# Two row groups of the array at once: spreads of the mLSTM maxima and neighbourhood scores issued in pairs

## The reference, cut to what matters

```python
# neighbourhood attention: 4 heads of 64; local scores with bias beside scores on the context
s_loc = jnp.einsum('bwhd,biwjhd->bhwij', q_r, k_win)
s_ctx = jnp.einsum('bwhd,bchd->bhwc', q_r, k_ctx)
s = jnp.concatenate([s_loc * scale + bias, s_ctx * scale], axis=-1)
p = jax.nn.softmax(s, axis=-1)

# mLSTM, 4 heads, forwards and backwards
d_log = jnp.where(tri, b[..., :, None] - b[..., None, :] + ic[..., None, :], -jnp.inf)
inter = b + m[..., None]
m_t = jnp.maximum(inter, jnp.max(d_log, axis=-1))
s = jnp.einsum('bhtk,bhsk->bhts', qc, kc) * jnp.exp(d_log - m_t[..., None])
num = a[..., None] * jnp.einsum('bhvk,bhtk->bhtv', C, qc) + jnp.einsum('bhts,bhsv->bhtv', s, vc)
h = num / jnp.maximum(jnp.abs(den), jnp.exp(-m_t))[..., None]
```

## Time and profile before

| | before |
|---|---|
| median of 3 runs | 1969.7 us (1965.51 to 1973.23) |
| the profiled execution | 1965.12 us |
| its span | 1963.2 us |
| TensorE busy | 1693.0 us, 86% |
| VectorE, ScalarE, GpSimd busy | 547.5, 325.3, 96.3 us |
| mean granted TensorE clock | 0.935 |

### The profile page before, as it was taken

The page is one execution under the profiler, slowest core; times in us unless marked ns, Lnnn a source line. Parts: engine busy times, 40 slices in busy tenths (PEclk is TensorE's granted clock), DMA queues, the critical chain, the costliest instruction groups (busy, mean ns, idle before and its releaser), DMA issues.

```text
span 1963.2 us, 21642 instructions
## 1 busy us (share of the span) xinstructions
PE 1693.0 (86%) x9155; PEld 881.1 (45%) x9155; DVE 547.5 (28%) x1054; ACT 325.3 (17%) x776; POOL 96.3 (5%) x171
## 2 busy tenths in 40 slices
PE   6999999999997998979888799999997766576765
PEld 2656444444476432424222266857885323222222
DVE  2145044354664121112111523334113111011102
ACT  4113143200023100101001321243012000000001
POOL 5000110000021100000000000110000000000000
PEclk9999999999998999999999899999998877777776
DMA  9310104544576799999999931104766999999995
GB/s 345 116 44 22 16 1 193 215 153 147 172 303 229 283 405 421 421 421 421 421 421 421 391 124 57 32 7 132 249 242 264 421 422 421 421 420 420 421 420 246
DMA packets 130668, 525.17 MB, mean 268 GB/s; under 512 B 9886, under 2 KB 73532, under 8 KB 75276
## 3 DMA queue, kind: packets, MB, share of 16 engines
q1 hardware_dynamic: 127884, 520.47, 67.1%
q0 software_dynamic: 2688, 3.32, 0.9%
HBM read 522.70 MB, written 1.05 MB: 267 GB/s over the span
## 4 chain that ended last, share of the span: by engine, by line
PE 60%; DMA 33%; DVE 4%; ACT 1%; issue 1%; SPq 0%; DVEq 0%; ACTq 0%
DMA ring<-in_w_e_dram 33%; PE ps L813 13%; PE ps L1073 9%; PE ps L1253 8%; PE ps L1082 4%; PE ps L1112 4%; PE ps L1037 3%; PE ps L723 2%; PE ps L1275 2%; PE ps L999 2%; PE ps L1205 2%; PE ps L915 2%; PE ps L1233 2%; PE ps L1021 1%; PE ps L892 1%
## 5 line engine op out<-in xcount | busy, mean ns | idle before, releaser
L1253 PE MATMUL ps<-ring,arena 128*32 128x256 f32 (+1 forms) x2880 | 381.1, 511 | 111.7 <-DMA ring<-in_w_e_dram 108.6
L1253 PEld LDWEIGHTS ps<-ring,arena 128*32 128x32 f32 (+1 forms) x2880 | 124.8, 130 | 354.1 <-DMA ring<-in_w_e_dram 179.7
L1275 PE MATMUL ps<-ring,arena 128*32 128x256 f32 (+1 forms) x1472 | 216.2, 564 | 74.0 <-DMA ring<-in_w_e_dram 70.3
L1073 PE MATMUL ps<-arena,ring 128*128 128x512 f32 (+1 forms) x576 | 191.8, 486 | 0.0
L813 PE MATMUL ps<-arena,ring 128*128 128x512 f32 (+1 forms) x480 | 175.2, 523 | 1.4 <-DVE arena L1828 1.4
L1275 PEld LDWEIGHTS ps<-ring,arena 128*32 128x32 f32 (+1 forms) x1472 | 69.6, 141 | 216.4 <-issue 111.0
L2054 DVE COPY arena<-ps 32x512 f32<-32x512 f32 (+1 forms) x128 | 70.9, 554 | 271.0 <-PE ps L1275 269.7
L1617 ACT ACTIVATE arena<-ps 128x512 f32<-128x512 f32 (+1 forms) x32 | 15.7, 490 | 777.1 <-PE ps L1253 777.1
L1073 PEld LDWEIGHTS ps<-arena,ring 128*128 128x128 f32 x576 | 109.1, 190 | 76.1 <-issue 68.6
L813 PEld LDWEIGHTS ps<-arena,ring 128*128 128x128 f32 x480 | 90.2, 190 | 82.5 <-issue 76.6
L2047 DVE TENSOR_TENSOR arena<-arena,ps 128x512 f32<-128x512 f32 (+1 forms) x32 | 17.7, 554 | 368.8 <-PE ps L1253 368.8
(11 more groups left out here) (215 smaller groups left out, 1435.3 us busy)
## 6 DMA issues: line engine op xcount, KB each, us to landing
ring<-in_w_e_dram SPq DMA_DIRECT2D x364, 1024.0 KB, 17.8
ring<-in_w_in_dram SPq DMA_DIRECT2D x44, 1024.0 KB, 9.0
ring<-in_w_mod_dram SPq DMA_DIRECT2D x40, 1024.0 KB, 11.2
arena<-in_w_e_dram SPq DMA_DIRECT2D x17, 1024.0 KB, 7.1
ring<-in_w_out_dram SPq DMA_DIRECT2D x8, 1024.0 KB, 11.4
arena<-in_w_mod_dram SPq DMA_DIRECT2D x8, 1024.0 KB, 14.7
arena<-in_w_br_ml_dram SPq DMA_DIRECT2D x8, 512.0 KB, 6.1
arena<-in_w_br_mla_dram SPq DMA_DIRECT2D x8, 256.0 KB, 3.9
```

The source lines that it names most:

```text
L1073: mm = pe.matmul(ps[:, u % 3, tq], wg[:, k, cols], hT[:, k, tq], start=k == 0, stop=k == KD - 1)
L1253: mm = pe.matmul(ps[M * j:M * j + M, m, 0:NW], XSTs[l][e // GROUP % 2][:, kk, e % GROUP, 0:M], w[:, k, j * NW:(j + 1) * NW], start=kk == 0 ...
L1275: mm = pe.matmul(ps[M * j:M * j + M, 3, 0:NW], lhs, w[:, k, j * NW:(j + 1) * NW], start=kk == 0, stop=kk == KD - 1)
```

## The change

Only TensorE's program changes. In the mLSTM loop `spread_m` now issues both directions of a head, each as a matmul over its own 32 rows instead of 64, one behind the other; a head's two spreads stand in front of the wait for `p_ready` of the odd map before, behind that map's projection. In the attention loop the MLA half keeps its order; in the neighbourhood half the scores of two heads are issued one behind the other (rows 0 to 63 and 64 to 127 of the array), then the two turns of the pair before, then the gate products of both units, then the values of the pair before. Both scores of a pair wait for both exponentials of the pair before.

```diff
                 def spread_m(u):
-                    h, d = L.pairs[u]
                     if u >= 2:
-                        pe.wait_ge(sem("e1_ready"), before("e1_ready", l) + 4 * (u - 1))
-                    r = 32 * d + h
-                    pe.matmul(ps[:, 3 + d, tq], ident[0:64, r:r + 1].to_broadcast([64, P]), R3[0:64, 2, tq],
-                              start=True, stop=True).then_inc(sem("nm_ready"), 1)
+                        pe.wait_ge(sem("e1_ready"), before("e1_ready", l) + 4 * u)
+                    h = L.pairs[u][0]
+                    for d in range(2):
+                        at = 32 * d
+                        pe.matmul(ps[:, 3 + d, tq], ident[at:at + 32, at + h:at + h + 1].to_broadcast([32, P]),
+                                  R3[at:at + 32, 2, tq], start=True, stop=True).then_inc(sem("nm_ready"), 1)
...
                 spread_m(0)
-                spread_m(1)
                 for u, (h, d) in enumerate(L.pairs):
...
+                    if d == 1 and u + 1 < len(L.pairs):
+                        spread_m(u + 1)
                     pe.wait_ge(sem("p_ready"), before("p_ready", l) + u + 1)
                     if d == 1 and h + 1 < HEADS:
                         scores_ml(h + 1)
                     values_ml(u)
-                    if u + 2 < len(L.pairs):
-                        spread_m(u + 2)
...
-                for i in range(nu + 2):
-                    if i < nu:
+                half = nu // 2
+                for i in range(half + 1):
+                    if i < half:
                         score(i)
-                    if i < nu:
                         gate_products(6 * KD * i // nu, 6 * KD * (i + 1) // nu)
-                    if 1 <= i <= nu:
+                    if i >= 1:
                         turn(i - 1)
                     if i >= 3 and i % 2:
                         values(i - 3)
+                for i in range(half, nu + 2, 2):
+                    if i < nu:
+                        pe.wait_ge(sem("attn_exp"), before("attn_exp", l) + i)
+                        score(i)
+                        score(i + 1)
+                    if i > half:
+                        turn(i - 2)
+                        turn(i - 1)
+                    if i < nu:
+                        gate_products(6 * KD * i // nu, 6 * KD * (i + 2) // nu)
+                    values(i - 2)
```

## The result

The changed kernel takes 1996.6 us (median of 4 runs, 1992.0 to 2000.3), the kernel before, on the same chip, 1968.1. The ratio is 1.015, 95% interval 1.0132 to 1.0169: slower by 28 us, where the forecast was +8 and the range ended at 1987. The profiled execution has a span of 1990.2 us, 27.0 over that of before, at a mean granted clock of 0.921 (0.935 before).

The account below looks back on a forecast made before the run. TensorE was taken to bound the kernel, transfers following it. mLSTM +7.2 and +6.5, attention -3.6 and -5.9, clock +4 sum to +8.2 on 1965.1: 1973.3, or 1978 for the median; range 1969 to 1987.

Parts of the forecast that it names:

- the overlap: Spreads and scores: two matmuls on different row groups run fully side by side, a spread pair costing 1.05 us.
- Rival 2: Paired matmuls don't overlap, 1983 us (chance 0.13), or take three passes of four, 1980.5 us (0.07).
- the stall, its place and its price: mLSTM loops: TensorE waits for VectorE's weighing three times per layer, 4.95 and 3.60 us; loops +7.2 and +6.5.
- attention: Neighbourhood half of the attention loop: paired scores save 5.9 us in layer 0 and 3.6 in layer 1.
- The chain through the exponential: Neighbourhood half: serial VectorE and ScalarE steps from score to second exponential bound latent pairs at 5.9 us, over TensorE's 5.65.
- the way to the end: Mixers to kernel end: every microsecond TensorE gains or loses moves later transfers too and is passed on whole.
- rival 3: A later stage waiting for transfers swallows the mLSTM delay while attention's 9.5 us gain stays: 1960 us, chance 0.05.
- the clock's term: mLSTM stalls: idle TensorE lowers the granted clock in three falls at 1.4 us, +4 us, bounds 0 and 10.
- Rival 4: Longer stalls still, the clock falling at all six mLSTM stalls: 1985 us or more, chance 0.05.

Follow-up runs that it names:

- e5: e1 with a turn between the two scores of a pair, from the second pair on; 1967.3 us, ratio 1.0007 to the kernel before.
- e3: Changed kernel plus useless 128-row matmuls between a pair's two spreads, filling the mLSTM stalls; 1972.8 us, ratio 1.0041 to the kernel before.
- e1: Kernel before with only the attention loop changed, its mLSTM loop left as before; 1954.4 us, ratio 0.995.
- e8: Changed kernel with spread pairs a projection earlier and VectorE taking both row maxima of a neighbourhood pair before normalising; 1948.6 us, ratio 0.9904.
- e6: As e3, with 1 and 2 useless matmuls per stall (layers 0 and 1) in place of 3 and 5; 1993.4 us, ratio 1.0137.
- e10: As e3, but the useless matmuls use 32 rows instead of 128, 4 and 6 per stall; 1987.8 us, ratio 1.0106.

## Why the prediction was wrong

- **Right: the overlap.** Pairs on different row groups run side by side; 1.06 for two spreads, 1.06 for two scores. Rival 2, in both its forms, is out: neither does a pair take twice one, nor three passes of four. e5 shows that attention's gain hangs on it.
- **Right: the stall, its place and its price.** Predicted 4.95 and 3.60 us; measured 4.96 to 5.01 and 3.60 to 4.00, ended by the weighing, three times in each layer. Without the clock the loops cost +6.8 and +6.4 (e3), forecast +7.2 and +6.5.
- **Right: attention.** -5.9 and -3.6 forecast, -5.9 and -3.6 in e1, whose clock is at full there (the changed kernel has -5.9 and -0.7, see the clock). The chain through the exponential bound the latent pairs at 5.78 us, forecast 5.9, and e8 shows that this chain was the bound, by 0.1 us where TensorE's work is longest and by 1.0 where it is shortest. That both sums agree to the tenth is in part luck: single pairs were 0.1 to 0.25 us shorter than forecast, and one stretch of low clock moves a stage by more.
- **Right: the way to the end.** All of it reached the end of the kernel, to within 3 us; rival 3 is out.
- **Wrong: the clock's term, "three falls at 1.4 us (part of each slow stretch is idle anyway): +4 us", and its bound of 10.** The direction was right and the size failed, by a factor of nearly six: of the 36.5 us that the mLSTM loops lost, 13.2 are waits and 23.3 are clock (e3). Both factors of the term were too small. The clock fell behind all six stalls, not three. And the price of one fall, taken as the time from the scores to the values of the next map less the same time in e3, was 4.6, 4.6 and 4.3 us in layer 0 and 1.6, 1.6 and 3.3 in layer 1, not 1.4. Two more falls of 1.7 and 1.6 us stand behind the waits before the values of maps 4 and 6 in layer 0 (the earlier trace rows has the first of these waits); before has the waits without the falls, and e1, with the loop of before, has one of the two.

The clock did not come back when TensorE went to work again: in layer 0 it stayed at half over 8.5 to 9.5 us of scores and values. I took the price from the earlier trace rows, where the idle of 2.89 us is followed by full-array work of another stage. Falls with only full-array work behind them cost near that here too: 1.6 us behind layer 1's first stall, 1.7 and 1.6 behind the two waits. The four dearest had scores on 64 rows in the slow stretch, but so had one that cost 1.6, and no run here shows that the scores are the reason. The earlier trace rows suggested that what counts is how long TensorE is idle. The same idle of 2.58 us with a fall behind it in eight traces and none in three, e6 (1.73 us of idle, same fall) and e10 (no idle, same fall) show that it is not that alone.

Rival 4 ("a fall at all six: 1985 or more") named the count and its open end holds the result, but its price was the same 1.7 us.

Three points stay open. Why the clock falls at the start of layer 1's attention in eight traces and not in before, e1 and e3: before, e1 and e5 have the same code ahead of it, and e5 has the fall. So the 2.9 us there can't be put down to the change, and the stage lengths of a single profile scatter by 2 to 3 us for such reasons. Why some falls last three times as long as others. And whether the 32-row spreads or the short idle behind them brought the fall in e6: e10 shows that few rows alone can do it in most cases, not that idle can't.

## What to carry to other kernels

Issuing two small matmuls on different row groups one behind the other gives the second for nothing; but to put them next to each other one of them has to move, and where it moves to decides: here one place made the two mLSTM loops 36.5 us longer, and the other, one projection earlier, made them 4.7 us shorter with the same instructions. When a wait is added, price the clock as well as the wait: take a full-speed and a half-speed time of the very work behind it, count a fall at every wait for the upper bound, and don't take one idle that passed at full clock as proof that such an idle is free. When a pair is issued at once, order its consumer's work in pairs as well, or the first one's later steps stand in front of the second one's first.

## What the runs showed of the hardware that I had not expected

- Matmuls on 32 rows did not hold TensorE's clock in five of e10's six filled stalls: in layer 0's first it fell to 1.2 GHz during 5.7 us of uninterrupted 32-row matmuls, while in e3 128-row matmuls in the same place left it at 2.4 GHz.
- Once down, it stayed down over the scores (64 rows) and most of the values, 124.0 to 133.5 us at 0.50, though TensorE was busy for 9.2 of these 9.5 us.
- Matmuls in float32 on different row groups interleave by pass: the first passes of both start together and the second passes follow together (120.92, and 121.45 and 121.46 in e10), although kernel.py issues the first matmul as a whole ahead of the second. The Trainium skill, TensorE: Matmul & The Clock Gate, Part 3, says that matmuls start and end strictly in program order; if the two passes of a matmul stand together in that order, which no trace here shows, a pair would by that have taken three passes, and here it took two (1.06 us).
- The same idle at the same place is not always followed by the same clock: 2.58 us before layer 1's first attention score, at 1.00 behind it in three traces, fallen in eight.
